# A weight ring of eight units, seven row buffers, and expert sums two ticks behind their dots

## The reference, cut to what matters

```python
def trunk(x, ...):
    for l in range(DEPTH):                                   # 2
        hn = rms_norm(x, norm1_w[l])
        proj = hn @ w_in[l]
        y_ssd = ssd_branch(...)                              # 8 groups, conv, two scans
        y_att = attention_branch(...)                        # 24 heads in 4 rounds
        merged = gates[:, :, 0] * (y_ssd @ w_ssd_out[l]) + gates[:, :, 1] * (y_att @ w_attn_out[l])
        x = x + merged @ w_out[l]
        x = x + peer_ffn(rms_norm(x, norm2_w[l]), w_query[l], sub_keys[l], expert_u[l], expert_v[l])
    return rms_norm(x, final_norm_w)

def block(args):                                             # inside peer_ffn: 128 experts per token
    xb, ib, gb = args
    hid = gelu(einsum('td,thkd->thk', xb, expert_u[ib]))     # 128 dots per token
    return einsum('thk,thkd->td', gb * hid, expert_v[ib])    # 128 weighted sums per token
```

## Time and profile before

| | |
|---|---|
| median of three runs | 4074.26 us |
| the profiled execution's own time | 4077.83 us |
| its span, first to last instruction | 4075.7 us |
| mixer of pass 0 (nothing beside it until its query) | up to about 640 us |
| mixers of passes 1, 2, 3 with expert ticks between | from there to about 3430 us |
| expert half of pass 3, alone | about 3430 to 4056 us |
| bytes moved | 1444.5 MB, mean 354 GB/s |

### The profile page before, as it was taken

How to read it: one execution, slowest core, us unless ns; L and a number is a source line. 1 busy time by engine, 2 the same in 40 slices (tenths; PEclk the granted TensorE clock), 3 DMA queues, 4 the chain that set the end, 5 groups by cost and what they waited for, 6 DMA issues and landing times.

```text
span 4075.7 us, 41582 instructions
## 1 busy us (share of the span) xinstructions
PE 3543.2 (87%) x13610; PEld 2369.9 (58%) x13610; DVE 2813.0 (69%) x5690; ACT 1843.9 (45%) x4797; POOL 1202.4 (30%) x1094
## 2 busy tenths in 40 slices
PE   7999997988999797988889787988989887778887
PEld 6876875666668564666667564666667562222222
DVE  3642128788777787788777788788778687655544
ACT  3642013676545324676435324676545323343333
POOL 1000002333333223333333224333333224433332
PEclk9999998999999899999999998999999988999999
DMA  6543447899999989999999989899999989999998
GB/s 199 171 163 127 151 141 294 346 395 388 392 420 417 422 309 374 353 399 403 392 424 417 423 305 374 342 405 409 385 421 417 422 301 384 427 427 427 427 427 358
DMA packets 252124, 1444.54 MB, mean 354 GB/s; under 512 B 31608, under 2 KB 31608, under 8 KB 118788
## 3 DMA queue, kind: packets, MB, share of 16 engines
q0 software_dynamic: 164976, 1133.94, 68.5%
q1 hardware_dynamic: 86800, 307.82, 20.2%
q10 hardware_dynamic: 132, 0.12, 0.0%
HBM read 1439.31 MB, written 7.13 MB: 355 GB/s over the span
## 4 chain that ended last, share of the span: by engine, by line
PE 29%; DMA 26%; DVE 24%; ACT 14%; issue 6%; POOL 0%; DVEq 0%; ACTq 0%; POOLq 0%
DMA rows<-in_w_uv,idx 25%; PE banks L577 15%; DVE rows L1433 7%; PE sums L836 5%; DVE x L1442 5%; ACT arena L900 4%; DVE arena L1242 3%; PE banks L836 3%; ACT diag L1035 1%; ACT L900 1%; ACT L1024 1%; PE banks L713 1%; ACT wgt L1028 1%; PE banks L634 1%; DVE arena L1268 1%
## 5 line engine op out<-in xcount | busy, mean ns | idle before, releaser
L544 POOL DMA_INDIRECT rows<-in_w_uv,idx x1024 | 1154.9, 1128 | 2221.7 <-DVE x L1442 1075.7
L1433 DVE CUSTOM_DVE_ANT_0 rows<-rows,xn 128x1024 f32<-128x1024 f32 x1024 | 1240.2, 1221 | 526.5 <-DMA rows<-in_w_uv,idx 524.9
L577 PE MATMUL banks<-hT,ring 128*128 128x256 f32 x6656 | 1485.5, 381 | 32.2 <-ACT arena L945 18.6
L577 PEld LDWEIGHTS banks<-hT,ring 128*128 128x128 f32 x6656 | 1260.4, 190 | 284.7 <-issue 81.4
L836 PE MATMUL sums<-rows,diag 128*128 128x512 f32 x1848 | 924.6, 633 | 166.0 <-ACT diag L1035 139.8
L1024 ACT ACTIVATE gelu<-hid 128x1 f32<-128x1 f32 x1024 | 205.6, 201 | 1365.1 <-DVE hid L1433 1361.6
L836 PEld LDWEIGHTS sums<-rows,diag 128*128 128x128 f32 x1848 | 352.5, 201 | 612.7 <-issue 302.8
L1442 DVE SCALAR_TENSOR_TENSOR x<-rows,wgt,x 128x1024 f32<-128x1024 f32 x434 | 555.9, 1281 | 14.6 <-ACT wgt L1028 14.6
L1242 DVE SCALAR_TENSOR_TENSOR arena<-banks,pr,arena 128x254 f32<-128x254 f32 (+1 forms) x512 | 245.4, 482 | 171.1 <-ACT arena L926 157.4
L1028 ACT ACTIVATE wgt<-gelu,gate 128x1 f32<-128x1 f32 x1024 | 301.6, 295 | 33.3
L836 PE MATMUL banks<-rows,diag 128*128 128x512 f32 x512 | 253.9, 618 | 62.4 <-ACT diag L1035 62.4
(11 more groups left out here) (161 smaller groups left out, 2509.2 us busy)
## 6 DMA issues: line engine op xcount, KB each, us to landing
ring<-in_w_ssd SPq DMA_DIRECT2D x192, 512.0 KB, 7.1
ring<-in_w_att SPq DMA_DIRECT2D x144, 512.0 KB, 7.8
ring<-in_w_mrg SPq DMA_DIRECT2D x128, 512.0 KB, 11.5
arena<-a_rows POOLq DMA_DIRECT2D x32, 1024.0 KB, 9.3
ring<-in_w_qry SPq DMA_DIRECT2D x64, 512.0 KB, 4.6
arena<-bias_tiles POOLq DMA_DIRECT2D x16, 1152.0 KB, 11.2
ring<-in_w_out SPq DMA_DIRECT2D x32, 512.0 KB, 17.9
rows<-in_w_uv,idx POOLq DMA_INDIRECT x1024, 12.8
```

What stands on the lines that cost most here:

```text
L544: nc.gpsimd.indirect_dma_start(out=rows[n % NB][:, :], out_offset=None, in_=w_uv, in_offset=bass.IndirectOffsetOnAxis(ap=idx[:, t, s:s + 1 ...
L577: mm = pe.matmul(out, w[:, k * P:(k + 1) * P], rhs[:, k0 + k, :], start=start and k == 0, stop=stop and k == n - 1)
L1433: v.tensor_tensor_reduce(u, u, xn2[:, (n // SLOTS_T) % 3, :], 1.0, 0.0, ALU.mult, ALU.add, hid[:, k:k + 1]).then_inc(u_done, 1)
```

## The change

RING goes from 6 to 8, NB from 8 to 7, LAG from 3 to 2. The memory stays the same: two more units of 4 KB a partition, one less row buffer of 8 KB. AHEAD stays 4. The list of units gets new skipped slots, so that units 6 to 8 of an att round stay neighbours in a ring of eight.

```diff
-RING = 6
-UNITS = ([("ssd", g, j) for g in range(GROUPS) for j in range(6)] + [("att", i, j) for i in range(4) for j in range(9)]
-         + [("mrg", c, j) for c in range(8) for j in range(5)] + [("out", 0, j) for j in range(8)]
-         + [None] * 2 + [("qry", 0, j) for j in range(16)])
+RING = 8
+UNITS = [("ssd", g, j) for g in range(GROUPS) for j in range(6)]
+for i in range(4):
+    UNITS += [("att", i, j) for j in range(6)]
+    UNITS += [None] * (-len(UNITS) % RING if len(UNITS) % RING > RING - 3 else 0)
+    UNITS += [("att", i, j) for j in range(6, 9)]
+UNITS += [("mrg", c, j) for c in range(8) for j in range(5)] + [("out", 0, j) for j in range(8)]
+UNITS += [None] * (-len(UNITS) % RING) + [("qry", 0, j) for j in range(16)]
...
-NB = 8
-LAG = 3
+NB = 7
+LAG = 2
 AHEAD = NB - LAG - 1
```

## The result

The changed kernel takes 4090.15 us (median of six runs, 4086.18 to 4097.86) against 4073.19 for the kernel before in the same set: a ratio of 1.0038, 95% interval 1.0028 to 1.0048, or +17 us between the medians and +15 by the ratio. A second set gave 1.0054 (1.0040 to 1.0068), +22 us. I had forecast no change, at 4072. The time lies inside my range and near the 4089 of rival C, which is in part luck: waits of C's kind are there, but the experiments show that they cost this much only together with a release of row buffers that I had priced at nothing.

The account below looks back on a forecast made before the run. No single engine was taken as the bound: DMA in the last 626 us and at mrg's end and out, PE, DVE and ACT waits elsewhere. Terms -6 - 2 + 4 + 2 = -2 us gave 4072; range 4054 to 4094, 8 in 10.

Parts of the forecast that it names:

- rival C: Inside ssd, PE's waits for diagonals reach ACT at L926, 21 times 0.7 to 0.8 us: +17, 4089 us; chance 0.22.
- The first zero: Gathers: the sum that frees a row buffer stays in tick k-1 of the plan, so the release costs 0.
- The second zero: Inside ssd, PE's added diagonal waits, 1 to 3.5 us at some eight places a pass, are taken up at the heads: 0.
- Rival E: Last half: seven buffers don't cover the gather, a slot takes 2.81 us: +92, so 4164 us; chance 0.03.
- Norm2: Second norm, passes 1 to 3: a sum ahead of the transposes, fast sums behind: -2.0 us each, -6 in all.
- Rival D: Transposes don't lift the clock: norm2 costs 1.7 and the starts 3.1, three times each: 4094 us; chance 0.06.
- The starts of the passes: Passes 1 to 3: one sum moves ahead of the transposes: -2 us in pass 1, 0 in passes 2 and 3.
- From ssd to att: Step to att, three times: DVE stands at sums, `weigh` starts later: bounds 0 and +2.4 us, taken 1.3, +4 in all.
- Inside ssd: Sums closer behind their weights make DVE wait at two places a pass, three passes: bounds 0 and +4.5, taken +2 us.
- My sign for C: If ssd takes longer by 5 us or more a pass, C is right and the 0 for PE's waits wrong.
- The ring: Ring of eight removes PE's 8.0 us of weight waits at mrg and out, off the path: 0, bound -8.0.
- The sum: Whole kernel: -6 - 2 + 4 + 2 = -2 us, giving 4072 us.

Follow-up runs that it names:

- e1: Changed kernel with the weight ring back at 6: lag 2, seven row buffers. 4085.63 us, 1.0029 of the kernel before.
- e16: Lag 2, eight buffers, ring 6, gathers four ticks ahead, but POOL waits for the sum seven slots back: 4090.67 us, 1.0041 of the kernel before.
- e9: Kernel before with lag 2, gathers still four ticks ahead (eight buffers, ring 6): 4065.48 us, 0.9979 of the kernel before.
- e20: Kernel before with ring 5, four diagonal tiles, lag 2, eight buffers, gathers four ticks ahead: 4082.82 us, 1.0017.
- e19: Kernel before with ring 5, four diagonal tiles, lag 3, nine buffers, gathers four ticks ahead: 4080.17 us, 1.0009.
- the pair on the ring of four: Kernel before with ring 4, gathers four ticks ahead: lag 3 with nine buffers, 1.0130, and lag 2 with eight buffers, 1.0126.
- e10: The changed kernel measured once more, unaltered, in another set: 4093.29 us, 1.0054 of the kernel before.
- e5: Changed kernel with the sums on DVE back at a lag of three, those on PE at two: 4135.54 us, 1.0143 of the kernel before.
- e3: Changed kernel with only six weight units in flight at the start of pass 0: 4088.74 us, 1.0035 of the kernel before.
- e4: Changed kernel with POOL's eight bias-tile spreads issued behind the first decay rows of pass 0: 4098.73 us, 1.0055 of the kernel before.
- e6: Changed kernel with the sums on PE back at a lag of three, those on DVE at two: 4129.49 us, 1.0123 of the kernel before.
- e8: Kernel before with POOL's eight bias-tile spreads issued one behind each group's decay rows of pass 0: 4057.08 us, 0.9956.
- e2: Kernel before with ring 8 and seven buffers, lag 3, so gathers go three ticks ahead: 4144.01 us, 1.0155.

## Why the prediction was wrong

**The step that failed** is the price of the shorter lag in the mixers. I had it at -2 us in all, with two zeros in the sum: "The release sits at the same place of the plan. I price it at 0" for the gathers, and "0, with rival C for the contrary" for PE's waits for diagonals. Lag and buffers alone (e1) cost 12 us, and 17 in e16. The runs show that neither zero is the whole loss by itself; it takes both.

The first zero. The release is in tick k-1 before and after, but a release is a moment, not a place. e16 and e9 differ in that wait alone and are 25 us apart (e1 and e9: 20), so one tick at this place has a price. And the moment did move. From 726 gathers of the three halves in each trace: before, the sum that frees the buffer ended 0.5 us behind the end of the dot of tick k-1 on average, and in after, e1 and e16 1.0 us behind. It was PE's sums that moved, from 0.6 us ahead of the end of that dot to 0.5 behind; DVE's moved by less than 0.1. Releases more than 3 us behind rose from 38 to 65, 63 and 66. I had looked for a loss by the buffer only in the last half, where the DMA engines are full, and found the right 0 there. In the mixers a gather takes 11.2 to 11.3 us to land (means over the halves of before), its dot comes 16 us after the issue on average, and yet over 200 dots start the moment the row is there.

The second zero. The added waits for ACT are in every kernel with a lag of two (6 us at each start of a pass, and the step to att, both below). With a tick of slack more at the release they cost little: e20 against e19, 3 us, and the pair on the ring of four is equal.

How the two work together can be read from DVE's waits between 640 and 3430 us (us in total, one trace each):

| kernel | lag, release | for rows | for weights of slots | together |
|---|---|---|---|---|
| before | 3, tick k-1 | 240.6 | 14.6 | 255.2 |
| after | 2, tick k-1 | 236.9 | 33.6 | 270.5 |
| e1 | 2, tick k-1 | 233.2 | 34.7 | 267.9 |
| e16 | 2, tick k-1 | 230.7 | 35.1 | 265.8 |
| e9 | 2, tick k-2 | 201.4 | 36.6 | 238.0 |
| e19 | 3, tick k-2 | 183.5 | 14.5 | 198.0 |
| e20 | 2, tick k-2 | 162.3 | 37.2 | 199.5 |

The shorter lag adds about 20 us of waits for weights in each pair. From e19 to e20 the waits for rows fall by 21 us, so the time that DVE stands at a sum is time in which the next rows land. From before to after, e1 and e16 they fall by only 4 to 10 us, and both together grow by 11 to 15 us, near the loss of 12 to 22. DVE isn't the limit everywhere, so this is an account and not a proof. By it the loss isn't longer waiting for rows, as one would expect from a late release alone; it is that with the tight release the rows don't come sooner for all the standing. A likely reason is that a sum which DVE or PE stands at holds up POOL's next gather too; no run tests that by itself.

Rival E was the only one that had the buffers in it, and was set in the wrong place: its 92 us for the last half were 0, and what one tick of slack is worth (e9, e16) shows in the mixers.

**Norm2**, -2 each: the first query projection moved against the norm's first DVE instruction (L1184, L1188 after) by -2.4, -1.6 and -0.8, so -5 in place of -6. Right in mechanism. Rival D's times did not come: the sum ahead of the transposes ran slowly, and those behind them fast, without other work between:

```profile
2355.23 3.78 PE L840 MATMUL sums<-rows,diag 128*128 128x512 f32 x4 [25.27 <-ACT diag L1039]
2358.80 2.85 PE L593 MATMUL banks<-cst,arena 128*128 128x128 f32 x16
2362.69 3.70 PE L840 MATMUL sums<-rows,diag 128*128 128x512 f32 x8 [1.04 <-DVE hT L1200]
```

In this trace the granted clock rose during the transposes (0.50 from 2355 to 2359 us, 0.72 to 2362, 1.00 behind), with a sum just ahead of them, so it can't say which of the two lifted it. For transposes alone there is only the earlier trace rows of the kernel before.

**The starts of the passes**, -2, 0, 0: measured at the small projection, again against the norm's first DVE instruction, -2.0, +0.3 and +0.7. The -2 is in part luck: in e1 and e10 the same place of pass 1 gives +0.7 and +0.6, and in e1 the sum ahead of the transposes took 3.78 us there, against 1.98 in after. Then 6 us are lost one projection later at the wait for the diagonal, three times. That was my 0 for "PE will add waits for diagonals": I had priced waits of 1 to 3.5 us inside ssd and not looked at the slots around DVE's chain for the decays.

**From ssd to att**, +1.3 each: `weigh` starts 2.3, 1.8 and 2.0 us later against DVE's last own instruction before the wait (L1290, L1294 after), inside my bound of 2.4, and PE's first projection products of att 1.3, 2.8 and 2.6 us later against its last projections ahead of the step. So the term was set somewhat low, and the +4 of e5's expectation too high. **Inside ssd**, +2 in all: in pass 2 from the small projection to att the delay grew by 4.9 us in after and 9.0 in e1, the missed 6 us and the step's 2 us included, part of them given back in between.

Rival C named waits for ACT and nearly the right time. It had them at L926 inside ssd, 0.8 us apiece, and without the buffers in it; e9 and e20 have such waits and not the loss. My sign for C, ssd longer by 5 us a pass, came in both of them too (5.9 and 5.1 us in pass 2), so it was no sign of what the whole kernel loses.

**The ring**, 0 (bound -8): PE's waits at mrg and out did vanish for nothing. The loss at the start was in no case of mine, since I took the first 680 us as untouched, though SP's loads change there first. It cost 6.6 us at the first heads (5.1 in e10); of this the end keeps about 4 (mean of the two sets of after 1.0046, of the three kernels e1, e3 and e16, with six units in flight at the start, 1.0035), but single sets don't tell that from 0 or 8.

**The sum** as measured: +12 to +17 from the lag with seven buffers (e1, e16), about +4 from the ring at the start, against +15 and +22 by the ratios of the two sets.

**What stays open.** Before and e1 have the same slack in ticks and differ by 12 us, while the mean issue is only 0.2 to 0.3 us later. The steep dependence shown by e5, e1 and e9 speaks for the release, the table of DVE's waits for both together; how the 12 us divide was not measured, and may have no single answer. A lag of three with a release in tick k-2 and gathers four ahead on the ring of six, the missing corner, was not run for want of memory; e19 and e20 stand in for it on a ring of five, where PE also waits 24 to 30 us for att's weights, which may hide a part. That e4 to e6 lost for the reasons given is read from their traces, not tested further.

## What to carry to other kernels

Count a buffer ring's slack in time at the release, not in positions: ask when the last reader of the buffer is really done, and what that reader waits for. A shorter lag between producer and consumer frees a buffer and adds waits; here the buffer was worth more as slack for the next fetch, which also hid those waits (e9, -9 us), than as memory for something else (after, +15 to +22). And when prefetch gets deeper, look at the first hundred microseconds, where it competes with everything that nobody tuned.

## What the hardware showed that I had not expected

- POOL issued seven DMAs of scattered rows in 7.55 us and was then held at the eighth for 22.5 us (28.0 with two more weight loads in flight, 34.9 in e4) with no semaphore to wait for. A small DMA behind them took 14.8 us for its round trip; with nothing ahead of it in the queue (e8), 2.3.
- A wait of 4.03 us on PE cost 6 us: the sum behind it took 3.52 us in place of 1.88, with the granted clock at 0.66 over those 5 us.
- One gather less in flight changes nothing where the DMA engines are full (426 GB/s, latency 15.1 to 12.6 us), and in the whole kernel costs about 1.5% (e2), with DVE's waits for rows up by 115 us.
